# Folded sums of eight rows kept to the end of a mixture-of-experts layer, and the strips of two weight transfers asked for separately

## The chip, the cores and the metric

The kernel runs on one core of one Trainium2 chip. The metric is the device time of one execution, in microseconds (us). All inputs, weights and outputs are float32.

## What is computed

One layer of a decoder for 256 prompt rows and 8 sample rows (264 in all), each of 1024 columns. Its first part (a short convolution and retention) takes the first 166 us and is not touched, apart from a table of constants. The rest is this, with 32 experts of which each row uses 4:

```python
logits = x @ w_router + b_router
gates = softmax(top_4(logits))
h = xb @ w_up[e] + b_up[e]                         # w_up[e] is 1024 x 2048, 8 MB
act = min(h_glu, 7) * sigmoid(1.702 * h_glu) * (clip(h_lin, -7, 7) + 1)
y_rows = act @ w_down[e] + b_down[e]               # w_down[e] is 1024 x 1024, 4 MB
h = h + sum over k of gates[k] * y[k]
y_out = h * rsqrt(mean(h * h) + 1e-6) * norm_final
```

The kernel also returns the states of the first part.

## The kernel before

**The stream of weights.** Each expert has four chunks of `w_up` ("u", 2 MB each) and two of `w_down` ("d", 2 MB each): 192 chunks (`LAST`) in the order u of expert n, then d of expert n - 1. They go through a ring of ten slots of 2 MB (`ring_all`, chunk s in slot s % 10). SyncE (SP) issues all these transfers, each as soon as TensorE (PE) has used what stood in the slot (`mm_done`), so that some 30 us of work always stands in the DMA queue. From expert 8 to the start of expert 28 two neighbouring chunks are one transfer of 4 MB (`pairs`, L569; 128 rows of 32 KB). Before and after these come single chunks (L582), then halves (L540), and the last expert's `w_down` comes in four parts of 1 MB (L575, rows of pieces of 2 KB). A transfer counts as landed when its semaphore has all 16 increments, from all DMA engines that carry it.

**An expert's work on PE.** `ups(n)` multiplies 64 gathered rows with `w_up[n]` in eight steps j (L1035). Between the steps stand the gathering for the next expert (L1009, L1017, L1027) and, after three of them, `combine(n - 2, c)`: it multiplies the gates, spread over the rows, with the expert's 64 results (`y_rows`) for rows 0 to 127 (c = 0), 128 to 255 (c = 1) and the 8 sample rows (c = 2). VectorE (DVE) adds what it gives to `h_tok` (L1887). `downs(n - 1)` follows (L1054).

**The eight sample rows.** For experts 0 to 25 (`FOLD` = 26) combine has a folded form for c = 2: the 1024 columns of the eight rows lie as 4 groups of 32 partitions by 2 x 128 columns, eight matmuls of 128 columns give them (L1095), and DVE adds them to a tile `sums` (L1884). At expert 26 eight matmuls with the identity bring `sums` back into plain rows (L1107), and from then on combine uses the plain form for c = 2, two matmuls of 512 columns on 8 rows (L1102). The biases' term `gates @ b_down` is added at experts 20 to 22 (`bias(c)`, L1140), for c = 2 in the plain form too.

**The end.** `downs_last` handles the last expert's `w_down` in two halves of columns, p = 0 and p = 1 (L1114, eight steps j each). combine(30, c) stands between the steps of p = 0; `combine_last(0, c)` (L1129) stands after steps 1 and 4 of p = 1 for c = 0 and 1, and after the last step for c = 2, followed by `combine_last(1, c)` for c = 0, 1, 2. DVE adds each (`add_last`, L1954). ScalarE (ACT) squares each half row (L1470), GpSimd (POOL) multiplies the left halves with `norm_final` (L652, once `g_fin` is loaded, L584) and takes the roots of the mean squares (`last_root`, L656, L658: first for c = 0, then for c = 1 and 2 together, once all three are squared). ACT scales the left halves (L1533), DVE the right ones (L1997), and SP stores three blocks (L596, L599).

Of the kernel before, what the change touches and what calls it, by code (L numbers as in the profile page):

```python
# [13 lines left out]
P = 128  # L14
# [33 lines left out]
PAIRED = (8, 28)  # L48
LAST = E * CPR
TOK = [(0, 128), (128, 128), (256, NS)]  # L50
# [7 lines left out]
def hybrid_layer(nc, x_prompt, x_sample, state_conv, state_ret, norm_mix, w_in, conv_w, ret_norm, w_out,  # L58
# [17 lines left out]
    with ExitStack() as top:  # L76
# [76 lines left out]

        pairs = [s for s in range(place["u", PAIRED[0], 0], place["u", PAIRED[1], 0], 2) if s % RING < RING - 1]
        signal, seen = [], [0] * RING
        for s in range(LAST):
            if s - 1 in pairs:
                signal.append(signal[s - 1])
                continue
            seen[s % RING] += 1  # L160
            signal.append((s % RING, 16 * seen[s % RING]))

        with ExitStack() as ph:
# [183 lines left out]
            gt = lay(6304, T)[P - E:P]  # L347
            g_fin = lay(5280, D)
# [6 lines left out]
            weighted = [h_rows[:, 0:512], h_rows[:, 512:1024], xg[0:NS, :]]  # L355
# [3 lines left out]
            early_in = sem("early_in")  # L359
# [29 lines left out]
            last_in = [sem(f"last_in{p}") for p in range(2)]  # L389
            fin_part = sem("fin_part")  # L390
            fin_eps = sem("fin_eps")
            weighed_again = sem("weighed_again")
            fin_redone = sem("fin_redone")
# [42 lines left out]
            FOLD = 26  # L436

            def ring(s):
                r = s % RING
                return ring_a[:, r, :] if r < FIRST else ring_b[:, r - FIRST, :]  # L440

# [9 lines left out]
            def half_signal(s):  # L451
                return s % RING, 16 * sum(h % RING == s % RING for h in halved if h <= s)

# [25 lines left out]
            def _(sp):  # L479
# [17 lines left out]
                for j in range(2, 2 * len(ORDER) + 4):  # L497
# [12 lines left out]
                    if j >= 3:  # L510
# [5 lines left out]
                        if j % 2 and k == STASHED:  # L516
                            sp.dma_start(ring_a[:, k, 0:2 * FF], chunk_src(stream[k])[:, 0:2 * FF]).then_inc(landed[k], 16)
                            sp.dma_start(ring_a[:, k, 2 * FF:4 * FF],
                                         chunk_src(stream[k + RING])[:, 2 * FF:4 * FF]).then_inc(early_in, 16)
# [34 lines left out]
                for s in range(RING, LAST):  # L554
# [23 lines left out]
                    if s in halved:  # L578
# [19 lines left out]
                sp.wait_ge(fin_rows, 3)  # L598
                sp.dma_start(y_sample.rearrange("b s d -> (b s) d"), h_tok[0:NS, 2, :]).then_inc(stored, 16)  # L599
                sp.wait_ge(stored, 48)  # L600
# [3 lines left out]
            def _(pool):  # L604
# [43 lines left out]
                pool.wait_ge(late_in, 32)  # L648
                for c in range(CT):
                    pool.wait_ge(comb_added, CT * (E - 1) + c + 1)  # L650
                    n = TOK[c][1]
                    pool.tensor_tensor(weighted[c], h_tok[0:n, c, 0:512], g_fin[0:n, 0:512],  # L652
                                       ALU.mult).then_inc(fin_weighted, 1)
                def last_root(c0, c1, i):
                    pool.wait_ge(fin_ssq, c1)
                    pool.tensor_tensor(st[:, 6 + c0:6 + c1], st[:, c0:c1], st[:, 3 + c0:3 + c1], ALU.add).then_inc(fin_chain, 1)  # L656
                    pool.wait_ge(fin_chain, i + 1)
                    pool.tensor_tensor(st[:, 6 + c0:6 + c1], st[:, 6 + c0:6 + c1],  # L658
                                       minus_half[:].broadcast_to([P, c1 - c0]), ALU.pow).then_inc(fin_scale, 1)

                pool.wait_ge(fin_eps, 1)
                last_root(0, 1, 0)
                last_root(1, CT, 1)

            @block.tensor
            def _(pe):
# [398 lines left out]
                def combine(n, c):  # L1065
# [19 lines left out]
                    else:  # L1085
                        pe.wait_ge(comb_added, CT + CT * n + c)
                        if c == 0:
# [3 lines left out]
                    if c == 2 and isinstance(n, int) and n < FOLD:  # L1091
                        for g in range(4):
                            for half in range(2):
                                at = slice(half * CAP, (half + 1) * CAP)
                                mm = pe.matmul(bank[32 * g:32 * g + 32, C + half, 0:P], spread[at, n % 2, t0:t0 + 32],  # L1095
# [971 lines left out]
```

## Time and profile before

| | |
|---|---|
| median of three runs | 1082.04 us (1081.49 to 1084.55) |
| the profiled execution, its own time | 1081.66 us |
| its span, first to last instruction | 1079.8 us |
| TensorE busy | 1065.2 us, 99% of the span |
| VectorE, ScalarE, GpSimd busy | 361.4, 152.8, 11.9 us |
| granted TensorE clock, mean of the span | 0.998 of full |
| weights and the rest moved by DMA | 431.47 MB, mean 400 GB/s |

The profiled execution's time is 1.86 us above its span, which is what lies around the instructions, and 0.38 us under the median of the three runs. A busy share of 99% doesn't tell that PE sets the time: its weights come at the pace of the DMA engines, and the stretches in which one or the other is ahead have to be read apart.

### The profile page before, as it was taken

Reading aid. Unit: us, or ns where it says so; the run is one execution under the profiler, and the core shown is the slowest. Engines: PE = TensorE matmul, PEld = TensorE weight load, DVE = VectorE, ACT = ScalarE, POOL = GpSimd, SP = SyncE. Lnnn points to the kernel's source line nnn. Section 1 sums busy time; section 2 is a strip of 40 time slices with the busy share of each in tenths; the row PEclk is TensorE's granted clock in tenths of the full one; section 3 lists DMA queues with packets and bytes.
Section 4 is the critical chain, followed back from the end, with each engine's and each line's share of the span. In section 5 each row is a group of like instructions: output and inputs, shape, how many; then the busy total and the mean of one; then the engine's idle time right before and its main releaser. Section 6 shows DMA issues by size and latency. Waiting matters only on the chain.

```text
span 1079.8 us, 13215 instructions
## 1 busy us (share of the span) xinstructions
PE 1065.2 (99%) x5687; PEld 445.8 (41%) x5688; DVE 361.4 (33%) x572; ACT 152.8 (14%) x302; POOL 11.9 (1%) x28
## 2 busy tenths in 40 slices
PE   9999999999999999999999999999999999999997
PEld 7888664333333333333333333333333333333332
DVE  3376534233322233332222233323232232232234
ACT  2121144111111101111111110011111101101113
POOL 1000010000000000000000000000000000000002
PEclk9999999999999999999999999999999999999999
DMA  8875969999999999999999999999999999999995
GB/s 291 305 276 199 402 214 390 419 425 426 427 429 433 431 430 429 433 427 434 429 429 429 434 431 430 429 429 432 433 432 427 432 430 433 423 427 428 424 413 188
DMA packets 45515, 431.47 MB, mean 400 GB/s; under 512 B 4968, under 2 KB 20364, under 8 KB 25872
## 3 DMA queue, kind: packets, MB, share of 16 engines
q1 hardware_dynamic: 44848, 430.41, 95.3%
q8 instruction: 46, 0.75, 0.3%
q10 hardware_dynamic: 608, 0.20, 0.1%
q14 instruction: 13, 0.11, 0.0%
HBM read 427.00 MB, written 3.48 MB: 399 GB/s over the span
## 4 chain that ended last, share of the span: by engine, by line
PE 87%; DMA 11%; issue 0%; ACT 0%; DVE 0%; POOLq 0%; DVEq 0%; ACTq 0%; POOL 0%
PE bank L1035 39%; PE bank L1054 16%; DMA ring_all<-in_w_up 10%; PE bank L716 9%; PE bank L1102 6%; PE bank L1009 4%; PE bank L1046 2%; PE bank L826 2%; PE bank L1017 2%; PE bank L1027 1%; PE bank L1095 1%; PE bank L669 1%; PE bank L1114 1%; DMA ring_all<-in_w_in 1%; PE bank L834 1%; PE bank L1140 1%
## 5 line engine op out<-in xcount | busy, mean ns | idle before, releaser
L1035 PE MATMUL bank<-ring_all,work 128*64 128x512 f32 x2040 | 482.9, 600 | 4.9 <-DMA ring_all<-in_w_up 4.9
L1035 PEld LDWEIGHTS bank<-ring_all,work 128*64 128x64 f32 x2040 | 133.9, 136 | 253.4 <-issue 243.9
L1054 PE MATMUL bank<-ring_all,work 128*64 128x512 f32 x992 | 225.3, 596 | 0.0
L1887 DVE TENSOR_TENSOR h_tok<-h_tok,bank 128x1024 f32<-128x1024 f32 (+1 forms) x67 | 81.7, 1220 | 234.2 <-PE bank L1102 228.3
L1054 PEld LDWEIGHTS bank<-ring_all,work 128*64 128x64 f32 x992 | 68.4, 137 | 128.1 <-issue 128.0
L716 PE MATMUL bank<-work,ring_all 128*128 128x264 f32 x384 | 87.1, 387 | 0.5 <-DMA ring_all<-in_w_in 0.5
L716 PEld LDWEIGHTS bank<-work,ring_all 128*128 128x128 f32 x384 | 72.3, 190 | 13.1 <-DMA ring_all<-in_w_in 1.1
L1857 DVE TENSOR_TENSOR work<-bank,bias_up 128x1024 f32<-128x1024 f32 x32 | 39.2, 1224 | 113.9 <-PE bank L1046 113.9
L1102 PE MATMUL bank<-work 64*128 64x512 f32 (+1 forms) x268 | 75.1, 637 | 0.0
L1874 DVE TENSOR_TENSOR work<-work 128x512 f32<-128x512 f32 x32 | 22.2, 692 | 106.5 <-ACT work L1453 106.4
L1437 ACT ACTIVATE work<-bank 128x264 f32<-128x264 f32 x32 | 12.5, 391 | 313.1 <-PE bank L1027 313.1
L1445 ACT ACTIVATE shared<-bank 128x512 f32<-128x512 f32 x64 | 34.7, 595 | 118.4 <-PE bank L1035 118.4
L1459 ACT ACTIVATE work<-bank 128x512 f32<-128x512 f32 x31 | 18.5, 597 | 218.3 <-PE bank L1054 218.3
L1009 PE MATMUL bank<-x_tok,pick_b 128*64 128x512 bf16 x372 | 45.6, 379 | 0.0
L1884 DVE TENSOR_TENSOR work<-work,bank 128x256 f32<-128x256 f32 x26 | 11.0, 421 | 90.4 <-PE bank L1095 90.4
L1102 PEld LDWEIGHTS bank<-work 64*128 64x128 f32 (+1 forms) x268 | 19.2, 177 | 53.1 <-issue 51.5
L1846 DVE TENSOR_TENSOR work<-bank,vec 128x512 f32<-128x512 f32 x31 | 21.4, 692 | 58.2 <-PE bank L1017 43.3
L1046 PEld LDWEIGHTS bank<-ident,shared 128*128 128x128 f32 x256 | 27.4, 141 | 25.9 <-ACT shared L1445 23.5
L1431 ACT ACTIVATE work<-bank 128x512 f32<-128x512 f32 x31 | 18.5, 597 | 125.4 <-PE bank L1009 125.4
L1009 PEld LDWEIGHTS bank<-x_tok,pick_b 128*64 128x64 bf16 x372 | 22.7, 110 | 29.8 <-issue 18.2
L1046 PE MATMUL bank<-ident,shared 128*128 128x128 f32 x256 | 35.0, 280 | 0.0
L1017 PEld LDWEIGHTS bank<-ident,work 128*128 128x128 f32 x124 | 17.4, 210 | 25.2 <-issue 25.2
(238 smaller groups left out, 550.6 us busy)
## 6 DMA issues: line engine op xcount, KB each, us to landing
ring_all<-in_w_up SPq DMA_DIRECT2D x40, 4096.0 KB, 33.5
ring_all<-in_w_down SPq DMA_DIRECT2D x20, 4096.0 KB, 34.5
ring_all<-in_w_up SPq DMA_DIRECT2D x33, 2048.0 KB, 15.2
ring_all<-in_w_down SPq DMA_DIRECT2D x15, 2048.0 KB, 18.4
ring_all<-in_w_up SPq DMA_DIRECT2D x29, 1024.0 KB, 10.4
ring_all<-in_w_down SPq DMA_DIRECT2D x18, 1024.0 KB, 11.9
ring_all<-in_w_in SPq DMA_DIRECT2D x13, 1024.0 KB, 5.0
ring_all<-in_w_out SPq DMA_DIRECT2D x4, 1024.0 KB, 11.6
```

The source lines that it names most:

```text
L716: mm = pe.matmul(bank[:, i % 4, 0:T], w_ring[:, slot, k, m % 2 * P:(m % 2 + 1) * P], xnt[:, k, :] if j else x_raw[:, k, :], start=(k == 0) ...
L826: mm = pe.matmul(bank[:, 2 * c + n, :], mix_in[:, k, c * P:(c + 1) * P], wo_slot[i][:, a, :], start=(late == 0 and a == 0), stop=(late == ...
L1009: mm = pe.matmul(bank[half * CAP:(half + 1) * CAP, X, :], marks, rows[:, half * 512:(half + 1) * 512], start=(i == 0), stop=(i == len(part ...
L1017: mm = pe.transpose(bank[:, X, j * P:(j + 1) * P], xg[:, j:j + 4 * P - 3:4], ident[:])
L1035: mm = pe.matmul(bank[half * CAP:(half + 1) * CAP, up_bank(n) + b, :].rearrange("q (k p) -> q p k", k=KT), x, src[half][:, b * 512:(b + 1) ...
L1046: mm = pe.transpose(bank[:, HT + j // 4, j % 4 * P:(j % 4 + 1) * P], h_rows[:, j * P:(j + 1) * P], ident[:])
L1054: mm = pe.matmul(bank[half * CAP:(half + 1) * CAP, Y, :], av[:, 2 * i + k, :], src[:, k * D + half * 512:k * D + (half + 1) * 512], start= ...
L1102: mm = pe.matmul(bank[0:m, at_bank + half, :], spread[at, n % 2 if isinstance(n, int) else 0, t0:t0 + m], y_rows[at, :], start=True, stop= ...
L1445: nc.scalar.activation(h_rows.rearrange("p (k b q) -> p b k q", k=KT, b=2)[:, b], bank[:, up_bank(n) + b, :].rearrange("p (k q) -> p k q", ...
L1857: tt(hb[:].rearrange("p h j s -> p j h s"), bank[:, HT:HT + 2, :].rearrange("p a (j h s) -> p (a j) h s", h=2, s=CAP), bias_up[:, e, :, :] ...
L1874: tt(out[:], sig[:], hb[:, 1], ALU.mult).then_inc(act_ready, 1)
L1887: tt(rows, rows, bank[0:m, b:b + 2, :], ALU.add).then_inc(comb_added, 1)
```

## The change

Four things change.

1. The eight sample rows stay folded for all experts. At expert 0 eight matmuls with the identity put the rows' own values into the folded sums; `bias(2)`, the last two experts and the overflow rounds use the folded form; the eight matmuls of expert 26 (L1107) are gone. The sum of squares over the four groups of partitions is taken by two matmuls of one column with a constant 128 x 128 matrix (`same_row`), at the very end of PE's program (`join_rows`).
2. At the end the order is (0,0), (0,1), (0,2), (1,2), (1,0), (1,1) for (p, c), and the first three stand after steps 1, 3 and 5 of p = 1. The prompt rows' two stores come as before; the sample rows are stored folded by four transfers of 8 rows x 2 x 128, two on SP and two on ACT. POOL no longer weighs the sample rows; DVE scales them in one instruction of 128 x 256.
3. `g_fin`, a folded copy of `norm_final` (four transfers of 8 rows) and `same_row` are loaded into the ring slot of chunk 186, after PE has used it, in place of `g_fin` alone in `work`.
4. Two transfers of 4 MB, those of steps 4 to 7 of experts 16 and 25, leave out the last 768 and 512 columns (3 and 2 KB of each row). These strips are asked for by three more transfers each, of 69, 57 and 2 rows.

```diff
+UNEVEN = {(16, 2): 768, (25, 2): 512}
+FEW_ENGINES = (slice(0, 69), slice(69, 126), slice(126, 128))
+LATE = LAST - 6
...
-            seen[s % RING] += 1
+            seen[s % RING] += 1 + (len(FEW_ENGINES) if s in uneven else 0)
...
-                        sp.dma_start(ring_all[:, s % RING:s % RING + 2, :].rearrange("p a n -> p (a n)"),
-                                     pair_src(stream[s])).then_inc(landed[s % RING], 16)
+                        pair = ring_all[:, s % RING:s % RING + 2, :].rearrange("p a n -> p (a n)")
+                        cut = 8 * FF - uneven.get(s, 0)
+                        sp.dma_start(pair[:, 0:cut], pair_src(stream[s])[:, 0:cut]).then_inc(landed[s % RING], 16)
+                        if s in uneven:
+                            for few in FEW_ENGINES:
+                                sp.dma_start(pair[few, cut:], pair_src(stream[s])[few, cut:]).then_inc(landed[s % RING], 16)
...
-                sp.wait_ge(comb_psum, CT * (FOLD + 1))
+                sp.wait_ge(mm_done, LATE + 1)
+                sp.dma_start(same_row, c_square[:, 8, :]).then_inc(late_in, 16)
                 sp.dma_start(g_fin[:], norm_final.rearrange("(a d) -> a d", a=1)
                              .partition_broadcast(P)[:, 0, :]).then_inc(late_in, 16)
+                for g in range(4):
+                    sp.dma_start(g_fold[32 * g:32 * g + NS], norm_final.rearrange("(a n g t) -> g a n t", a=1, n=2, g=4)[g]
+                                 .partition_broadcast(NS)[:, 0]).then_inc(late_in, 16)
...
-                pool.wait_ge(late_in, 32)
-                for c in range(CT):
+                pool.wait_ge(late_in, 112)
+                for c in range(2):
...
-                    if c == 2 and isinstance(n, int) and n < FOLD:
+                    if c == 2:
...
-                            if p == 1 and j in (1, 4):
-                                combine_last(0, j // 4)
-                    combine_last(0, 2)
-                    for c in range(CT):
-                        combine_last(1, c)
+                            if p == 1 and j in (1, 3, 5):
+                                combine_last(j // 2)
+                    for i in range(CT, 2 * CT):
+                        combine_last(i)
...
+                pe.wait_ge(late_in, 112)
+                pe.wait_ge(fin_part, CT)
+                pe.wait_ge(fin_sel, 1)
+                join_rows()
```

On SP, in the middle of the stream, each expert had three transfers of 4 MB before (`ring_all` is the ring, 128x8192 a pair of chunks, line 569): two of `w_up`, one of `w_down`. This stands for expert 16 with the change (line 584 is what line 569 was, line 587 is new):

```order
L584 DMA ring_all<-in_w_up 128x8192
L584 DMA ring_all<-in_w_up 128x7424
L587 DMA ring_all<-in_w_up 69x768
L587 DMA ring_all<-in_w_up 57x768
L587 DMA ring_all<-in_w_up 2x768
L584 DMA ring_all<-in_w_down 128x8192
```

Expert 16's second pair has lost 768 columns, and three transfers behind it bring them; all four count on the pair's semaphore.

On PE, the second half of the last expert (L1114 is `down_last`, L1129 `combine_last`), before:

```order
L1129 MATMUL bank<-work 128x256 [waits comb_added]
L1129 MATMUL bank<-work 128x256
L1114 MATMUL bank<-ring_all,work 64x256 x6
L1129 MATMUL bank<-work 8x256 [waits comb_added]
L1129 MATMUL bank<-work 8x256
L1129 MATMUL bank<-work 128x256 [waits spread_copied,y_copied,comb_added]
L1129 MATMUL bank<-work 128x256
L1129 MATMUL bank<-work 128x256 [waits comb_added]
L1129 MATMUL bank<-work 128x256
L1129 MATMUL bank<-work 8x256 [waits comb_added]
L1129 MATMUL bank<-work 8x256
```

and with the change (L1137 is `down_last`, L1154 and L1159 `combine_last` for the sample and the prompt rows, L1311 the join):

```order
L1154 MATMUL bank<-work 32x128 [waits comb_added]
L1154 MATMUL bank<-work 32x128 x3
L1137 MATMUL bank<-ring_all,work 64x256 x4
L1154 MATMUL bank<-work 32x128 [waits spread_copied,y_copied,comb_added]
L1154 MATMUL bank<-work 32x128 x3
L1159 MATMUL bank<-work 128x256 [waits comb_added]
L1159 MATMUL bank<-work 128x256
L1159 MATMUL bank<-work 128x256 [waits comb_added]
L1159 MATMUL bank<-work 128x256
L1311 MATMUL bank<-work,ring_all 128x1 [waits fin_sel,fin_part,late_in]
L1312 MATMUL bank<-work,ring_all 128x1
```

The sample rows' first combine has moved ahead of the last two steps, their second to the front of the last three, and the join stands behind all.

On SP, the end of the program before (the last weights, `norm_final`, the load of the greatest count, and the stores behind the branches of the overflow rounds):

```order
L575 DMA ring_all<-in_w_down 128x4x512 x4
L584 DMA work<-in_norm_final 128x1024
L459 TENSOR_LOAD most
...
L596 DMA out<-h_tok 128x1024 x2
L599 DMA out<-h_tok 8x1024
```

and with the change:

```order
L592 DMA ring_all<-in_w_down 128x4x512 x4
L601 DMA ring_all<-in_c_square 128x128
L602 DMA ring_all<-in_norm_final 128x1024
L605 DMA ring_all<-in_norm_final 8x2x128 x4
...
L617 DMA out<-h_tok 128x1024 x2
L620 DMA out<-work 16x1x128 x2
```

Five loads have come behind the last weights on this queue, and two short stores stand where one was; ACT has two more like them at its end.

## Rows read from the trace of the kernel before

**Rows 1.** The page: the span, the engines' busy time.

```profile
span 1079.8 us, 13215 instructions
PE 1065.2 (99%) x5687; PEld 445.8 (41%) x5688; DVE 361.4 (33%) x572; ACT 152.8 (14%) x302; POOL 11.9 (1%) x28
```

**Rows 2.** Sums by stretch: bounds, length, busy time by engine, clock, DMA share, GB/s.

```profile
650.00:850.00 200.00, 198.60 (x1045) 69.67 (x1041) 59.59 (x87) 22.33 (x42) 0.00 (x0) 1.00 1.00 431
```

**Rows 3.** The waits of PE: line, releaser, total us, times, longest.

```profile
PE bank L1035 <- DMA ring_all<-in_w_up: 4.9, 5, 1.2
```

**Rows 4.** PE in order of time, experts' first steps: start, length, what, idle.

```profile
857.82 3.65 PE L1035 MATMUL bank<-ring_all,work 128*64 128x512 f32 x16 [1.18 <-DMA ring_all<-in_w_up]
...
916.10 3.65 PE L1035 MATMUL bank<-ring_all,work 128*64 128x512 f32 x16 [1.18 <-DMA ring_all<-in_w_up]
```

**Rows 5.** The chain that ended last, one piece: start, length, what.

```profile
877.79 38.17 DMA ring_all<-in_w_up
```

**Rows 6.** Line 575 in 1030 to 1032 us: the transfer, and its time to landing.

```profile
L575 SPq DMA_DIRECT2D ring_all<-in_w_down x1: 3189/3189/3189, 1030.5 to 1030.5; - x1
DMA to landing us min/median/max: 27.0/27.0/27.0
```

**Rows 7.** Sums by stretch at the end of the stream, columns as in rows 2.

```profile
1059.00:1060.00 1.00, 1.00 (x8) 0.30 (x6) 0.26 (x1) 0.00 (x0) 0.00 (x0) 1.00 1.03 395
1060.00:1061.00 1.00, 1.00 (x10) 0.48 (x8) 0.96 (x1) 0.00 (x0) 0.00 (x0) 1.00 0.78 301
...
1062.00:1063.00 1.00, 1.00 (x10) 0.36 (x8) 1.00 (x1) 0.00 (x0) 0.00 (x0) 1.00 0.59 219
...
1065.00:1066.00 1.00, 1.00 (x10) 0.45 (x6) 0.00 (x0) 0.19 (x1) 0.00 (x0) 1.00 0.29 115
1066.00:1067.00 1.00, 1.00 (x12) 0.60 (x10) 0.69 (x1) 0.00 (x0) 0.00 (x0) 1.00 0.00 0
```

**Rows 8.** PE in order of time: the forms of combine and bias.

```profile
616.45 0.45 PE L1095 MATMUL bank<-work 64*32 64x128 f32 x16
616.83 1.94 PE L1035 MATMUL bank<-ring_all,work 128*64 128x512 f32 x8
...
791.90 1.88 PE L1140 MATMUL bank<-h_tok,work 32*8 32x512 f32 x4
793.71 1.09 PE L1046 MATMUL bank<-ident,shared 128*128 128x128 f32 x8
...
961.45 1.03 PE L1102 MATMUL bank<-work 64*8 64x512 f32 x4
962.41 1.91 PE L1107 MATMUL bank<-work,ident 128*8 128x128 f32 x16
964.26 1.94 PE L1035 MATMUL bank<-ring_all,work 128*64 128x512 f32 x8
```

**Rows 9.** All engines in order of time, the end: start, length, what, idle.

```profile
1057.55 1.08 PE L1114 MATMUL bank<-ring_all,work 128*64 128x256 f32 x8
...
1067.13 1.29 POOL L652 TENSOR_TENSOR shared<-h_tok,work 128x512 f32<-128x512 f32 x1 [905.17 <-DVE h_tok L1954]
...
1069.71 2.69 PE L1129 MATMUL bank<-work 64*8 64x256 f32 x16
...
1070.36 2.17 DVE L1954 TENSOR_TENSOR h_tok<-h_tok,bank 8x512 f32<-8x512 f32 x3 [1.29 <-PE bank L1129]
...
1073.53 0.63 ACT L1470 ACTIVATE work<-h_tok 8x512 f32<-8x512 f32 x1
...
1074.60 0.70 POOL L658 TENSOR_TENSOR work<-work,minus_half 128x2 f32<-128x2 f32 x1
...
1075.33 1.40 DVE L1997 SCALAR_TENSOR_TENSOR h_tok<-h_tok,work 128x512 f32<-128x512 f32 x2 [0.96 <-POOL work L658]
...
1076.76 0.35 SPq L599 DMA_DIRECT2D out<-h_tok  x1
```

More of the change, by code:

```diff
@@ L154, in hybrid_layer @@
         pairs = [s for s in range(place["u", PAIRED[0], 0], place["u", PAIRED[1], 0], 2) if s % RING < RING - 1]
+        uneven = {place["u", e, j]: cols for (e, j), cols in UNEVEN.items()}
         signal, seen = [], [0] * RING
@@ L597, in _ @@
                 sp.wait_ge(fin_ready, 3)
-                sp.wait_ge(fin_rows, 3)
-                sp.dma_start(y_sample.rearrange("b s d -> (b s) d"), h_tok[0:NS, 2, :]).then_inc(stored, 16)
-                sp.wait_ge(stored, 48)
+                for g in range(2):
+                    sp.dma_start(y_folded(g), sums[32 * g:32 * g + NS]).then_inc(stored, 16)
+                sp.wait_ge(stored, 96)
                 sp.wait_ge(out_done, 16 * 3)
@@ L1090, in combine @@
                         pe.sem_inc(pe_passed, 1)
-                    if c == 2 and isinstance(n, int) and n < FOLD:
+                    slot = n % 2 if isinstance(n, int) else 0
+                    if c == 2:
+                        if isinstance(n, int) and n == 0:
+                            for g in range(4):
+                                for half in range(2):
+                                    pe.matmul(bank[32 * g:32 * g + 32, C + half, 0:P], ident[0:NS, 0:32],
+                                              h_tok[0:NS, 2, half * 512 + g * P:half * 512 + (g + 1) * P], start=True, stop=False)
                         for g in range(4):
@@ L1139, in bias @@
                     for half in range(2):
-                        mm = pe.matmul(bank[0:m, C + half, :], gt[:, t0:t0 + m], b_down_sb[:, half * 512:(half + 1) * 512],
-                                       start=True, stop=True)
+                        if c == 2:
+                            for g in range(4):
+                                mm = pe.matmul(bank[32 * g:32 * g + 32, C + half, 0:P], gt[:, t0:t0 + 32],
+                                               b_down_sb[:, half * 512 + g * P:half * 512 + (g + 1) * P], start=True, stop=True)
+                        else:
+                            mm = pe.matmul(bank[:, C + half, :], gt[:, t0:t0 + m], b_down_sb[:, half * 512:(half + 1) * 512],
+                                           start=True, stop=True)
                     mm.then_inc(bias_psum, 1)
@@ L1468, in square_part @@
                 def square_part(p, c, done):
[L1469 to L1470 removed]
+                    rows = sums[:, p, :] if c == 2 else h_tok[:, c, p * 512:(p + 1) * 512]
+                    nc.scalar.activation(sig[:].rearrange("p j s -> p (j s)")[:, 0:P if c == 2 else 512], rows,
                                          ACT.Square, scale=D ** -0.5,
[L1472 removed]
+                                         accum_out=st[:, 3 * p + c:3 * p + c + 1]).then_inc(done, 1)
                 for n in range(E):
@@ L1892, in add_bias @@
                     dve.wait_ge(comb_added, CT * (BIAS + c - 2) + c + 1)
-                    rows = h_tok[0:m, c, :].rearrange("p (a b) -> p a b", a=2)
-                    tt(rows, rows, bank[0:m, C:C + 2, :], ALU.add).then_inc(bias_added, 1)
+                    if c == 2:
+                        tt(sums, sums, bank[:, C:C + 2, 0:P], ALU.add).then_inc(bias_added, 1)
+                        return
+                    rows = h_tok[:, c, :].rearrange("p (a b) -> p a b", a=2)
+                    tt(rows, rows, bank[:, C:C + 2, :], ALU.add).then_inc(bias_added, 1)
                 nc.vector.memset(st[:], 0.0)
@@ L1980, in overflow @@
                     activate(n, None)
-                    for c in range(CT):
-                        add(CT + CT * n + c, c)
+                    for i, c in enumerate(LASTS):
+                        add(CT + CT * n + i, c)
                 def weigh_again(k):
                     dve.wait_ge(comb_added, k * CT + SUMS)
-                    dve.wait_ge(fin_weighted, CT)
-                    for c in range(CT):
+                    dve.wait_ge(fin_weighted, 2)
+                    for c in range(2):
                         ins = weigh(c)
```

194 lines of the change are left out of this document (109 added, 85 removed).

## The prediction

> **What bounds the kernel now.** The page comes first: PE is busy 99% of the span [rows 1]. That looks like a kernel bound by PE. The sums by stretch say something else as well: the DMA engines' share is 1.00 and they move 431 GB/s [rows 2], so PE and DMA are both full. Which is ahead decides what a saving is worth, so I read the waits of PE: five waits for `w_up`, 4.9 us in all, 1.2 at most [rows 3]. In order of time, experts 25 and 27 start 58.28 us apart, at 857.82 and 916.10, each just after such a wait [rows 4]: 29.14 us for an expert's 12 MB (12.58e6 bytes) is 432 GB/s, the DMA's own rate. So in this stretch the stream sets the pace, and PE catches up with it each time; the chain that ended last goes through such a transfer, 38.17 us long and asked for at 877.79 [rows 5]. After 916 no wait is shown. But the first part of the last `w_down`, asked for at 1030.5, takes 27.0 us to land, that is until 1057.5 [rows 6], and PE begins its step at 1057.55 [rows 9]. So there, 22 us before the end, the stream is still level with PE. A saving on PE ahead of 1057.5 is given back by a wait for weights, unless the stream gets earlier too. What comes behind 1057.55 is a tail of small work, one engine handing over to the next, and there each saving counts.
>
> The stream's end shows how the 16 engines stand. Their share is full until 1060, 0.78 in the next us, 0.59 from 1062 to 1063, 0.29 from 1065 to 1066, and nothing after 1066 [rows 7]. 0.59 of 16 is nine engines: some seven are done between 1060 and 1062, nine between 1064 and 1066.5. Each transfer is cut evenly among them, yet it counts as landed only with the last one. So seven engines lead by 4 to 6 us, and the lag of the rest is lost time for PE.
>
> **The change part by part.** The sum is made against the profiled execution, 1081.66 us, which is 0.38 under the median.
>
> The folded form costs 616.83 - 616.45 = 0.38 us on PE, the plain one 962.41 - 961.45 = 0.96 [rows 8]: 0.58 less for each of experts 26 to 30, 2.9 in all. The unfolding of expert 26 took 964.26 - 962.41 = 1.85, `bias(2)` 793.71 - 791.90 = 1.81 against some 0.4 now. Expert 0 gets eight short matmuls more, about as many columns as a folded combine, so 0.4 at most. Sum 2.9 + 1.9 + 1.4 - 0.4 = 5.8 us of PE, all but the 0.58 of expert 30 ahead of 1057.55. What hides them is the stream: if it didn't get earlier they would turn into waits, and I count them as nothing. Without that cover they would be worth 5.2 us.
>
> The strips. Per engine the rate is 431 / 16 = 26.9 GB/s. 3 KB of 128 rows are 393 KB, 24.6 KB or 0.91 us for each of 16 engines; 2 KB are 0.61 us. If the strips go to engines that lead, the others land everything behind the second strip 1.52 us earlier. The leaders pay. 128 rows go to 16 engines as eight each; if an equal share of rows is what makes the split, 69 and 57 rows can only go to three engines (23 and 19 each) and 2 rows to two. The pieces are small: with pieces of 2 KB the stream runs at 395 GB/s [rows 7], 24.7 per engine. So (393 + 262) / 3 / 24.7 = 8.8 us, less the 1.5 that they are spared, is 7.3 us more on each of three engines. Their lead is 4 to 6 us as rows 7 show it, and more in truth, since the last transfers were let into the queue late (the issue of the first of them took 3.2 us [rows 6], against 0.35 of line 599 [rows 9]) and the leaders ran dry. So after both strips the three are about the last ones: with a lead of 8 the stream's end comes 0.7 earlier, with 6 it comes 1.3 later. The bounds for this term are -1.5 (all the lead is there) and +1.3. I take -0.5, a lead just under 8, between the two, since the dry queue cuts off what rows 7 can show of it.
>
> The Trainium skill, "DMA: Bandwidth & Descriptors", section "Why a DMA increments its semaphore by 16 and not by 1", states that the number of engines is the largest one up to 16 that divides the slowest dimension on both sides, and that SP's transfers use the lowest-numbered ones. By that 69 and 57 rows go to three engines and 2 rows to two, always the same ones, which would make the sum above; by its "Rules for kernel authors", parts of a transfer that each spray over all 16 gain nothing, which would make it zero. No row here shows which engines lead.
>
> Issuing six more transfers takes SP time that nobody waits for; some 30 us of work stand in the queue.
>
> The tail, from the last step of PE on. Before: PE's last four combines start at 1069.71 and end at 1072.40, DVE's three first adds run 1070.36 to 1072.53 and the fourth follows, ACT's last square starts at 1073.53, POOL's last root runs 1074.60 to 1075.30, DVE scales 1075.33 to 1076.73, SP's last store is issued at 1076.76 and the span ends 3.0 later [rows 1, 9]. Now the first sample combine lies between two steps (+0.2 on PE, four matmuls in place of eight) and no longer behind them, and expert 30's is 0.58 shorter: the last step ends 0.4 earlier. Behind it come a short combine (0.2), a short add (under 0.4, 128 x 128) and then the two prompt blocks. DVE has three adds in place of four, the one on the chain short: the last add that POOL's second root needs ends 2.4 us after the last step in place of 3.5. ACT's square of the sample rows, 0.63 and 0.2 for the sum before, no longer stands behind the other two. So the second root ends 1.1 us earlier relative to the step. Behind it DVE has 0.7 for block 1 as before, and 0.4 in place of 0.65 for the samples. Then two stores of the samples on SP one after the other, and two on ACT beside them: this costs one issue more, 0.35 to 0.8 us (line 599 took 0.35). Net behind the last step: 0.3 to 1.1 earlier, I take 0.9. With the 0.4 the tail gives -1.3.
>
> Price of the new waits: the join on PE waits for `late_in`, with nothing behind it but the branch; its two matmuls of one column and the add on DVE end before ACT's second square does. POOL's first weighing (1.29 us a block, started at 1067.13 before, when DVE's first sum was there [rows 9]) waits for five more loads, which land behind the last weights, about 1067; its two blocks are done before 1070, and the root behind them is not due before 1071, so there's 1 us of slack.
>
> Sum: 0 - 0.5 - 1.3 = -1.8, so 1079.9 for the profiled time, 1080.2 for the median.
>
> **The rivals.**
> 1. The strips fall on engines that lag. Nothing in the rows excludes it: nine of sixteen lag. Then the last engine's stream ends up to 7.3 us later, and PE first waits for it at expert 26, behind the second strip. Less the tail's 1.3, and up to 2 us where a strip's engine isn't quite the last one, it's 4 to 6 us slower: 1084.4 to 1086.5, say 1086. It decides once one of the strips' engines leads by less than 3.5 us. Chance 0.17.
> 2. The strips change nothing, since they are shared out over all engines or the lead is just eaten up: only the tail remains, 1080.7; where the leaders end 1.3 later, 1082.0. Chance 0.25.
> 3. The full lead is there: stream -1.5, tail -1.3 to -1.6, so 1078.6 to 1079.2. The folded sums then also show, since PE needs them to keep up. Chance 0.15.
> 4. The tail gets worse: late loads or four short stores whose landings queue up, +1 to 1.5 in place of -0.9. Near 1082. Chance 0.05.
>
> **How the numbers follow.** The forecast (gain of 1 to 2.5 us) has 0.38. A change of under 0.3%, 3.2 us, can't be told from none by measuring this kernel. Within it lie the forecast, rivals 2 and 4 and most of rival 3; faster needs rival 3 in full and some of the runs' own spread (0.13); slower is rival 1 and a little of 2 (0.19). The range leaves out half of rival 3's lower part and the slower part of rival 1: 1078.4 to 1085.6.
>
> **What would show it.** Sums by stretch behind 1060: a share that stays near 1 longer and falls within 2 us, the end at 1065 to 1066, would show that the strips went to leaders. PE's waits for `w_up` at experts 20 to 25 shorter or no longer between waits (starts at 857 in place of 857.82), and possibly one longer at expert 26 or 27. No line for the unfolding; all c = 2 combines of 0.38. Waits of PE for weights also behind 1000, where none are now: the 5.8 us given back. From the first step of the last `w_down` to the end 21.0 us in place of 22.3. The prediction is wrong if that step starts later than 1058.5 (rival 1), or if the tail isn't shorter.

## The result

The changed kernel takes 1089.97 us (median of 6 runs, 1089.01 to 1091.4) beside 1081.51 us for the kernel before (6 runs, 1080.96 to 1084.55): ratio 1.0071, 95% interval 1.0057 to 1.0084. It is slower by 8.5 us. The forecast was 1080.2, a gain, with a range of 1078.4 to 1085.6; the measured time lies above the range, and "slower" had been given a chance of 0.19.

The page of the changed kernel: the span, the engines' busy time, and the traffic in 40 equal slices of 27.2 us:

```profile
span 1088.9 us, 13396 instructions
PE 1064.6 (98%) x5771; PEld 448.2 (41%) x5772; DVE 356.1 (33%) x574; ACT 151.4 (14%) x301; POOL 11.0 (1%) x27
GB/s 284 307 276 208 407 214 364 422 425 427 427 429 432 431 429 432 430 433 429 431 432 428 378 432 432 428 432 429 434 431 428 424 405 426 427 427 428 423 402 174
```

The span is 9.1 us longer than in [rows 1]. PE isn't busier (1064.6 beside 1065.2), its idle time grew from 14.6 to 24.3 us. Two slices drop out of a level of about 430 GB/s, the 23rd (378, from 599 us) and the 33rd (405, from 871 us): the places of the two strips. Next the waits of PE, then two pieces of PE in order of time (start, length, what, idle before), then four sums by stretch (columns as in [rows 2]), all of the changed kernel:

```profile
PE bank L1058 <- DMA ring_all<-in_w_up: 12.3, 9, 4.8
PE bank L1137 <- DMA ring_all<-in_w_down: 0.8, 1, 0.8
```

```profile
877.26 3.42 PE L1058 MATMUL bank<-ring_all,work 128*64 128x512 f32 x8 [4.77 <-DMA ring_all<-in_w_up]
...
1066.24 1.08 PE L1137 MATMUL bank<-ring_all,work 128*64 128x256 f32 x8 [0.78 <-DMA ring_all<-in_w_down]
```

```profile
596.00:612.00 16.00, 16.00 (x82) 5.68 (x80) 6.22 (x10) 1.71 (x3) 0.00 (x0) 1.00 1.00 337
...
874.00:876.00 2.00, 0.00 (x0) 0.00 (x0) 0.00 (x0) 0.00 (x0) 0.00 (x0) 1.00 1.03 330
876.00:878.00 2.00, 0.74 (x4) 0.29 (x6) 0.00 (x0) 0.00 (x0) 0.00 (x0) 0.89 0.83 347
878.00:880.00 2.00, 2.00 (x8) 0.38 (x4) 0.00 (x0) 0.00 (x0) 0.00 (x0) 0.50 1.18 508
```

For comparison, the first stretch in the kernel before:

```profile
596.00:612.00 16.00, 16.00 (x82) 5.42 (x78) 4.32 (x7) 1.71 (x3) 0.00 (x0) 1.00 1.00 429
```

The waits for `w_up` went from 4.9 us [rows 3] to 12.3, and one alone, at expert 25's strip, is 4.77. During the 16 us around the first strip the DMA share stays at 1.00 but the traffic is 337 GB/s; in the same stretch of the kernel before it is 429. The engines have work all the time and each piece takes longer: (429 - 337) x 16 / 431 = 3.4 us of the stream are lost.

At the second strip, from 868 to 884 us, the traffic is 367 in place of 431. The trace's records of single pieces show that the others are slowed too, and all of them: from 600 to 604 us each piece of 32 KB took 1.89 to 2.09 us, where it took 1.22 before the strip. The pair's semaphore got 24 increments in the trace, 16 for the large transfer and eight for the strip, as three, three and two engines would give.

Behind the wait of 4.77 us the granted clock is 0.50 of full, the lower of the two levels, and the next eight matmuls take 3.42 us, where the same step takes 1.94 in [rows 8]. The first step of the last `w_down` starts at 1066.24 in place of 1057.55 [rows 9]: 8.7 of the 9.1 us are there, ahead of the tail. The remaining 0.4 is the tail, 22.66 from that step to the end in place of 22.25.

### The profile page after: what moved, and what is told of

It reads as the page before. It is cut to its first block, busy times and chain, and to the rows that moved or that the text cites. A ratio compares the mean times of both kernels' runs of the same rounds, so it can differ in the third digit from the quotient of the medians.

```text
span 1088.9 us, 13396 instructions
## 1 busy us (share of the span) xinstructions
PE 1064.6 (98%) x5771; PEld 448.2 (41%) x5772; DVE 356.1 (33%) x574; ACT 151.4 (14%) x301; POOL 11.0 (1%) x27
## 4 chain that ended last, share of the span: by engine, by line
PE 81%; DMA 17%; SPq 0%; issue 0%; DVE 0%; POOLq 0%; ACT 0%; POOL 0%; DVEq 0%; ACTq 0%
PE bank L1058 35%; PE bank L1077 15%; DMA ring_all<-in_w_up 14%; PE bank L739 9%; PE bank L1130 5%; PE bank L1032 4%; DMA ring_all<-in_w_down 3%; PE bank L1069 2%; PE bank L849 2%; PE bank L1040 2%; PE bank L1050 1%; PE bank L1124 1%; PE bank L692 1%; PE bank L1137 1%; PE bank L857 1%; SPq L553 0%
## 5 line engine op out<-in xcount | busy, mean ns | idle before, releaser
L1058 PE MATMUL bank<-ring_all,work 128*64 128x512 f32 x2040 | 485.0, 602 | 12.4 <-DMA ring_all<-in_w_up 12.3
L1937 DVE TENSOR_TENSOR h_tok<-h_tok,bank 128x1024 f32<-128x1024 f32 x62 | 75.7, 1221 | 227.1 <-PE bank L1130 227.1
L1130 PE MATMUL bank<-work 64*128 64x512 f32 x248 | 70.2, 643 | 0.0
L1130 PEld LDWEIGHTS bank<-work 64*128 64x128 f32 x248 | 18.9, 186 | 50.2 <-issue 48.6
```

Source lines behind the costliest of these rows:

```text
L1058: mm = pe.matmul(bank[half * CAP:(half + 1) * CAP, up_bank(n) + b, :].rearrange("q (k p) -> q p k", k=KT), x, src[half][:, b * 512:(b + 1) ...
L1130: mm = pe.matmul(bank[:, at_bank + half, :], spread[at, slot, t0:t0 + m], y_rows[at, :], start=True, stop=True)
L1937: tt(rows, rows, bank[:, b:b + 2, :], ALU.add).then_inc(comb_added, 1)
```

## The experiments

Sixteen kernels were run. They are told by what they separate. The numbers in parentheses are a ratio to the kernel before and its 95% interval. The kernel before was timed again beside each group of them, with medians of 1082.58 to 1083.42, so the ratios compare better than the times do.

### Folding without strips, and strips without folding

```diff
-UNEVEN = {(16, 2): 768, (25, 2): 512}
+UNEVEN = {}
```

> The change without its strips (all 4 MB transfers whole). Theory A: the strips carry the whole loss and the folded sums change nothing but the tail, which the changed kernel shows 0.4 us longer (22.66 against 22.25 us from the first step of the last w_down): the stream sets that step's start as before, so +0.4 us, 1081.9, within 0.3%. Theory B (my prediction's sum): the tail is 1.3 us shorter, 1080.2. Rival C: the folded sums themselves cost the stream time (four small loads of 8 rows, a table of constants): over 1085.

Measured 1082.29 (1.000, 0.999 to 1.0011). Two lines of its page and its waits of PE:

```profile
PE 1060.5 (98%) x5771; PEld 446.6 (41%) x5772; DVE 356.0 (33%) x574; ACT 151.4 (14%) x301; POOL 11.0 (1%) x27
...
PE bank L1058 <- DMA ring_all<-in_w_up: 8.0, 9, 1.2
PE bank L1137 <- DMA ring_all<-in_w_down: 0.8, 1, 0.8
PE bank L1077 <- DMA ring_all<-in_w_down: 0.6, 1, 0.6
```

PE is busy 4.7 us less than in [rows 1], and waits 9.4 us for weights in place of 4.9: the saving is there and is given back, but for 0.2 us. The strips alone, put into the kernel before (the same `UNEVEN`, `FEW_ENGINES` and three transfers):

> The kernel before with the strips alone. Theory A: both strips slow the whole stream, 3.5 and 2.3 us on the mean of the engines as the changed kernel shows, and the three engines that take them end later than the last did: the last w_down's first step starts near 1066.2, 8 to 9 us later than before, 1090. Rival: the strips only shift load between engines, 1081.5 to 1083. Beside each strip the traffic should fall to 140 to 310 GB/s for some 8 us.

Measured 1090.23 (1.0066, 1.0042 to 1.0091), traffic of 324 GB/s from 596 to 612 us, and

```profile
PE bank L1042 <- DMA ring_all<-in_w_up: 11.4, 7, 4.8
```

So the strips are the whole loss. One strip only, in the changed kernel:

```diff
-UNEVEN = {(16, 2): 768, (25, 2): 512}
+UNEVEN = {(16, 2): 768}
```

> The kernel after with the strip of (25, 2) left away: (25, 2) is one whole transfer again, (16, 2) keeps its 3 KB strip by 69, 57 and 2 rows. If the two strips cost by their own delays alone (3.5 and 2.3 us of mean landing time of the 16 engines), 1085.5 to 1087.5. If what costs is mainly that a second loss meets a stream without a lead (the wait of 4.77 us at expert 25, then a clock of 0.57), 1083 to 1085.

Measured 1085.3 (1.0031, 1.0018 to 1.0045). The first strip costs 3.4 us by its ratio, as much as the stream lost in those 16 us; the second, though smaller, the other 4.3. That lies between the two expectations: most of the loss adds up, and the second strip costs some 2 us more than the 2.3 by which it delays the mean landing. The slow matmuls behind the long wait (1.5 us more than usual in the row above) may be a part of that. This was not separated further.

### What it is in the strips

The first experiments varied how the strip is cut up. All of these are the kernel before with strips of 3 and 2 KB at the same two pairs: by one transfer of all 128 rows (all16), by two of rows 0 to 63 and 64 to 127 (halves), by two of 119 and 9 rows (seven), and by the three of 69, 57 and 2 rows, but read from one contiguous stretch (contig):

```diff
 three kernels, with FEW_ENGINES in place of the slices of 69, 57 and 2 rows:
+FEW_ENGINES = (slice(0, 128),)                   # all16
+FEW_ENGINES = (slice(0, 64), slice(64, 128))     # halves
+FEW_ENGINES = (slice(0, 119), slice(119, 128))   # seven
 and with 69, 57 and 2 rows, read from one contiguous stretch of w_up (contig):
+source = w_up[0, stream[s][1], 0:width // 2, :].rearrange("r n -> (r n)").rearrange("(p w) -> p w", w=width)
```

> The same strips (the last 3 and 2 KB of each row), asked for by one transfer of 128 rows each, so that they are cut over all engines, eight rows each. Theory R (reading): pieces that lie 32 KB apart in memory are what slows everybody, whoever asks: traffic falls beside the strips as in the changed kernel, and the loss is some 3 to 6 us. Theory W (few engines): it is that three engines carry 43 small pieces each: then nothing is lost here but the price of small pieces, under 0.3 us, and the time is that of before, 1081.5.

> The strips by 69, 57 and 2 rows into the same places, but read from one contiguous stretch of the same expert's w_up (so these columns hold other weights; nothing else is changed). Theory R: with the pieces side by side in memory the traffic doesn't fall, and what stays is the overload of three engines: 1082 to 1084. Theory W: the same loss as with the strips where they belong, 1089 to 1090.

> [...] Theory P (place): it is writing outside the own eight rows that slows all: traffic falls beside the strips, for about 1 us a strip since the pieces are few, and pieces take 0.2 us in place of 0.12. Theory F (few): it is that the small pieces fall on few engines; then nothing changes against the transfer of 128 rows: pieces of 0.12 us, the time of before, 1082.

> The strips by transfers of 119 and 9 rows. If the equal split of rows holds, seven engines take 17 rows each and nine take one row: some 27 KB (1.0 us) and 18 KB (0.7 us) more for each of the seven leaders, which lead by more than 2 us. Without contention the other nine land 1.4 us earlier and the time falls by 1 to 1.5 us, 1081. With contention as in the strips of three engines (pieces of 0.2 us, all others slowed): each piece falls on 7 engines at once, the stretch is 17 pieces long (3.5 us) and the stream loses 1 to 3 us a strip: 1083 to 1087.

Sums by stretch from 596 to 612 us, in the order all16, contig, halves, seven:

```profile
596.00:612.00 16.00, 16.00 (x82) 5.46 (x80) 4.02 (x6) 1.71 (x3) 0.00 (x0) 1.00 1.02 435
...
596.00:612.00 16.00, 16.00 (x84) 5.52 (x78) 5.52 (x10) 1.71 (x3) 0.00 (x0) 1.00 1.01 345
...
596.00:612.00 16.00, 16.00 (x82) 5.56 (x80) 5.00 (x9) 1.71 (x3) 0.00 (x0) 1.00 1.01 349
...
596.00:612.00 16.00, 16.00 (x84) 5.42 (x80) 5.16 (x9) 1.71 (x3) 0.00 (x0) 1.00 1.00 343
```

The times were 1082.34 (1.0, 0.9987 to 1.0013), 1090.9 (1.0076, 1.005 to 1.0101), 1087.36 (1.0045, 1.0028 to 1.0061) and 1089.86 (1.0071, 1.0052 to 1.0089). A strip asked for by one transfer of 128 rows costs nothing, so small pieces as such are harmless. Reading from a contiguous stretch changes nothing. And halves cost too, though all 16 engines carry each of them (48 increments in the trace for the pair and the two halves of its strip): fewness of engines can't be all of it. The strips by 119 and 9 rows cost more than was expected of them, 1089.86 beside 1083 to 1087.

Then whole rows of 32 KB, to take the small pieces out altogether: 112 rows by the main transfer, 9 and 7 by two more.

```diff
+UNEVEN = {(16, 2): 112, (25, 2): 112}
+FEW_ENGINES = (slice(112, 121), slice(121, 128))
...
+first = uneven.get(s, P)
+sp.dma_start(pair[0:first], pair_src(stream[s])[0:first]).then_inc(landed[s % RING], 16)
```

> No strips of columns: the same two pairs are asked for as 112 rows (seven for each of 16 engines) and then 9 and 7 whole rows of 32 KB, so seven engines carry one row more than the even share and seven one row less, in pieces of 32 KB. Theory S (small pieces do the harm): traffic stays at 431 GB/s and the laggards land 2.4 us earlier after both; the time falls by up to 2 us if the leaders take the rows, 1080. Theory P or F: traffic falls beside the 16 rows as it does beside the strips, packets of 32 KB take over 1.5 us in place of 1.22, and the time is 1082 to 1086.

Measured 1122.16 (1.0365, 1.0347 to 1.0383): five times the loss of the strips, with big pieces only, where 1086 had been the most expected. The traffic there is half of what it was:

```profile
590.00:610.00 20.00, 20.00 (x104) 7.37 (x102) 6.22 (x10) 2.80 (x5) 0.00 (x0) 1.00 1.02 211
```

What all costly kernels share, and the harmless one doesn't, is that a transfer covers only a part of the 128 rows of the ring, and so cuts them in another place. That gave theory P: it matters to which rows (partitions) an engine writes. Suppose that rows are dealt out in order, in equal shares; no view shows which engine writes which rows, so this is an assumption. Then a transfer of 128 rows gives engine k rows 8k to 8k + 7 each time. Two transfers of even and odd rows leave every engine in its eight. Two halves don't (engine k gets rows 4k to 4k + 3, then 64 + 4k to 64 + 4k + 3), at the same count of transfers, bytes and pieces. Both were tried on the strips, and on the two whole pairs of 4 MB, (16, 2) and (25, 2), with no strips and all pieces of 32 KB:

```diff
 the strips:
-FEW_ENGINES = (slice(0, 64), slice(64, 128))
+FEW_ENGINES = (slice(0, 128, 2), slice(1, 128, 2))
 whole pairs of 32 KB rows, halves, then even/odd:
+PARTS = (slice(0, 64), slice(64, 128))
+PARTS = (slice(0, 128, 2), slice(1, 128, 2))
...
+for half in PARTS if s in uneven else (slice(0, P),):
+    sp.dma_start(pair[half], pair_src(stream[s])[half]).then_inc(landed[s % RING], 16)
```

> The kernel before with both strips asked for by two transfers of 64 rows, the even rows and the odd rows, instead of rows 0 to 63 and 64 to 127. [...] Theory P (it costs when an engine writes rows that are another engine's in the whole transfers): 1081.5 to 1083, within 0.1% of the kernel before, and 3 KB packets of about 121 ns with traffic near 431 GB/s. Rival N (two transfers more, or packets of 4 rows for each engine, cost by their number): as the halves, 1087 to 1088.

> [...] Theory P: those 4 MB move at about half the rate, as in the kernel with 112 + 9 + 7 rows (205 to 221 GB/s), some 9 to 10 us lost at each pair, 1095 to 1120. Rival U (it was the unequal count of rows per engine, 9 beside 7, and the few engines of the small transfers): none of that is left here, 1081.5 to 1084.

> [...] Theory P: within 0.15% of the kernel before, traffic stays near 431 GB/s through both pairs. Rival N (the number of transfers or their rows per engine costs): as the whole halves.

Strips by even and odd rows: 1082.11 (0.9994, 0.9981 to 1.0007). Whole pairs by halves: 1114.87 (1.0294, 1.0267 to 1.0321), by even and odd rows 1082.76 (0.9994, 0.9978 to 1.001). Sums by stretch: 596 to 612 us of the strips by even and odd rows, then 590 to 610 of the whole halves, then of the whole even and odd rows:

```profile
596.00:612.00 16.00, 16.00 (x81) 5.44 (x78) 4.42 (x6) 1.71 (x3) 0.00 (x0) 1.00 1.02 434
```

```profile
590.00:610.00 20.00, 18.74 (x96) 6.84 (x92) 6.48 (x10) 2.80 (x5) 0.00 (x0) 1.00 1.01 215
```

```profile
590.00:610.00 20.00, 20.00 (x116) 7.05 (x114) 6.22 (x10) 2.80 (x5) 0.00 (x0) 1.00 1.01 433
```

Same bytes, same number of transfers and pieces, 215 against 433 GB/s.

### Writing or reading, and which rows

The halves also differ from the even and odd rows in where in DRAM each transfer reads. So writing and reading were crossed (in `PARTS` the rows written stand first, the rows read second):

```diff
 to_halves:
+PARTS = ((slice(0, 64), slice(0, 128, 2)), (slice(64, 128), slice(1, 128, 2)))
 to_even_odd:
+PARTS = ((slice(0, 128, 2), slice(0, 64)), (slice(1, 128, 2), slice(64, 128)))
...
+sp.dma_start(pair[half], pair_src(stream[s])[rows_in_w]).then_inc(landed[s % RING], 16)
```

> The kernel before with two pairs asked for by two transfers of 64 rows, written to rows 0 to 63 and 64 to 127, but read from the even and the odd rows of the weights (the weights of two experts' steps so stand in other rows, and the output for them is another one). If what costs is where the rows are written: as the whole halves, 1110 to 1117, 590 to 610 us at about 215 GB/s. If it is how DRAM is read: as the kernel before, 1081 to 1084, 431 GB/s.

> The other way round: written to the even and the odd rows, read from rows 0 to 63 and 64 to 127 (here too the weights of two experts' steps stand in other rows). Writing decides: 1081 to 1084, 431 GB/s. Reading decides: 1110 to 1117, 215 GB/s.

Written to halves 1114.48 (1.0293, 1.0254 to 1.0332), written to even and odd rows 1082.64 (0.9995, 0.9984 to 1.0006). From 590 to 610 us, in this order:

```profile
590.00:610.00 20.00, 20.00 (x116) 7.08 (x114) 6.22 (x10) 2.80 (x5) 0.00 (x0) 1.00 1.00 215
```

```profile
590.00:610.00 20.00, 20.00 (x104) 7.41 (x102) 6.45 (x10) 2.80 (x5) 0.00 (x0) 1.00 1.01 432
```

Where the rows are written decides, where they are read makes no difference (half rows against even and odd ones). Why it does has two forms left: an engine leaves its own eight rows, or one transfer reaches only some of the places through which rows are written. The Trainium skill has the second form: "SBUF — State Buffer", section "Door 1: The DMA port swizzle", gives the 128 partitions to 16 ports in groups of four rows, with row p and row p + 32 on the same one and row p + 64 on another. By it rows 0 to 63 reach eight ports and even rows all sixteen, which would halve the rate in the one and leave it in the other; the 215 and 433 GB/s measured here agree. Rows 32 to 95 also reach all sixteen, but by the assumption above they lie as far from each engine's eight as a half does:

```diff
+PARTS = (slice(32, 96), slice(0, 32), slice(96, 128))
```

> The kernel before with two pairs asked for whole by transfers of rows 32 to 95, then 0 to 31, then 96 to 127. The Trainium skill, 'SBUF - State Buffer', section 'Door 1: The DMA port swizzle', lays partitions on 16 ports of which rows 0 to 63 reach eight and rows 32 to 95 all sixteen. Theory of ports: the first 2 MB of a pair move at about 431, the other 2 MB at about 215 GB/s; half of what the whole halves lost, so 1094 to 1101. Theory of an engine's own eight rows (rows 8k to 8k+7): in rows 32 to 95 the engines are as far from their own rows as in the halves, so all 4 MB go at 215 and it comes to 1110 to 1117.

Measured 1102.13 (1.0183, 1.0159 to 1.0207): 1.1 us above the interval of the ports (1094 to 1101), 8 under that of an engine's own eight (1110 to 1117). Sums by stretch of this kernel, then of the whole halves:

```profile
589.00:592.00 3.00, 3.00 (x18) 1.01 (x16) 0.42 (x1) 1.06 (x2) 0.00 (x0) 1.00 1.04 448
...
613.00:616.00 3.00, 2.59 (x6) 0.77 (x8) 0.00 (x0) 0.00 (x0) 0.00 (x0) 0.57 1.04 448
```

```profile
589.00:592.00 3.00, 3.00 (x16) 0.83 (x12) 0.08 (x1) 1.08 (x2) 0.00 (x0) 1.00 1.03 229
...
613.00:616.00 3.00, 0.00 (x0) 0.00 (x0) 0.00 (x0) 0.00 (x0) 0.00 (x0) 0.50 0.87 218
```

The halves are slow from about 588 until 616 us, 28 us for 4.2 MB that would need 19.5 us at half rate; the middle version only from 592 until 612. The semaphores' increments say the same engine by engine. The seven engines that lead took 9.8 us for their share of the first 2 MB as rows 0 to 63 (first increments at 588.5 and 598.3 us), but 4.9 us as rows 32 to 95 (588.6 and 593.5), which is the full rate.

Why the slow stretch is longer than the pair is read from the same increments: in the halves' kernel the first engine enters the pair at 588.5 us and the last one leaves it at 617.3, since up to 9 us lie between the first and the last engine's end of one transfer. While one engine is still in the pair, the pieces of all the others, who are already in the next whole transfer, are slow as well. For the same reason, it seems, the middle rows got less than their full gain: the nine engines behind needed some 7 us for them, while the leading ones were already in rows 0 to 31.
Last, the strips by three engines as in the change, but with rows spread over nearly the whole tile:

```diff
-FEW_ENGINES = (slice(0, 69), slice(69, 126), slice(126, 128))
+FEW_ENGINES = (slice(0, 114, 2), slice(1, 114, 2), slice(114, 128))
```

> The kernel before with the two strips asked for by 57 even rows of 0 to 112, 57 odd rows of 1 to 113 and rows 114 to 127: the first two go to three engines (19 rows each) as the 69 and 57 rows did, but each is spread over nearly all rows. Theory of writing place alone: within 0.2% of the kernel before, 596 to 612 us above 410 GB/s. If three engines alone cost: as the strips of 69, 57 and 2 rows, 1088 to 1091, 324 to 345 GB/s in that stretch. In between if both do.

Measured 1086.42 (1.0046, 1.0031 to 1.0061), 354 GB/s from 596 to 612 us beside 337 of the changed kernel. It fits neither theory, it lies between: some two thirds of the loss (0.46 of 0.66 to 0.71%) stay when the rows are spread. The ports alone don't explain this, nor the strips of the change: by the map three engines write through three ports at a time at most, yet from 600 to 604 us each 32 KB piece of the other transfers took 1.70 to 1.85 us here and 1.89 to 2.09 us in the changed kernel, 1.22 otherwise. So it is shown that strips cut this way slow the whole stream; by which path three engines slow all the others stays open.

### The tail

In the changed kernel the second sample combine, moved between two steps, no longer stands behind the last step. PE in order of time at that place, with ACT's copy that it waits for:

```profile
1077.31 1.08 PE L1137 MATMUL bank<-ring_all,work 128*64 128x256 f32 x8
...
1078.44 0.38 ACT L1509 ACTIVATE work<-bank 128x256 f32<-128x256 f32 x1 [0.94 <-PE bank L1137]
...
1078.92 0.42 PE L1154 MATMUL bank<-work 64*32 64x128 f32 x8 [0.53 <-issue]
```

PE's first combine behind the steps needs `y`, which ACT copies after the last step; in the kernel before, combine (0, 2) lay over this copy, now PE idles 0.53 us. So that combine was put back behind the last step, in the kernel without strips:

```diff
-if p == 1 and j in (1, 3, 5):
-    combine_last(j // 2)
+if p == 1 and j in (1, 4):
+    combine_last(j // 4)
...
-for i in range(CT, 2 * CT):
+for i in range(CT - 1, 2 * CT):
```

> The change without strips, with the third combine of p = 0 put back behind the last step of p = 1 (and the two others after steps 1 and 4, as before). Theory: in the changed kernel PE stands 0.5 us behind the last step since the next combine waits for ACT's copy of y, and the third combine, which used to fill this gap, costs 0.6 us between the steps. Put back, the tail from the first step of the last w_down is 0.5 us shorter than without strips (22.7): 22.1 to 22.2. Rival: the stores behind it set the end, nothing changes. The times alone can't tell: 1081.5 to 1082.5.

Measured 1082.03 (0.9995, 0.9985 to 1.0005). In its profile the first step of the last `w_down` begins at 1061.14 and the span ends at 1083.3: 22.16 in place of 22.66, as expected. Against the kernel before (22.25) this is next to nothing: the second root ends 0.7 us earlier after that step, and the stores take it back. The end of the changed kernel, all engines in order of time:

```profile
1081.88 0.55 POOL L678 TENSOR_TENSOR work<-work,minus_half 128x1 f32<-128x1 f32 x1
...
1082.69 1.08 POOL L678 TENSOR_TENSOR work<-work,minus_half 128x2 f32<-128x2 f32 x1
1083.28 1.68 SPq L617 DMA_DIRECT2D out<-h_tok  x2
...
1083.81 0.75 DVE L2053 SCALAR_TENSOR_TENSOR h_tok<-h_tok,work,ring_all 128x512 f32<-128x512 f32 x1 [0.59 <-POOL work L678]
1084.48 0.48 DVE L2060 SCALAR_TENSOR_TENSOR work<-work,ring_all 128x256 f32<-128x256 f32 x1
1084.99 2.36 ACTq L1584 DMA_DIRECT2D out<-work  x2
1085.00 1.52 SPq L620 DMA_DIRECT2D out<-work  x2
```

## Why the prediction was wrong

**Stream and PE are level until 1057.5, and a saving on PE is given back.** Right. 4.7 us less of PE work, 4.5 us more of waits, time unchanged (1.000).

**The size of the saving, 5.8 us.** It was 4.7 by the busy time; the term was worth nothing either way.

**The strips, -0.5 with bounds -1.5 and +1.3.** This is the step that failed: "(393 + 262) / 3 / 24.7 = 8.8 us, less the 1.5 that they are spared, is 7.3 us more on each of three engines", and above all what stood unsaid beside it, that the other thirteen go on at 26.9 GB/s each and "land everything behind the second strip 1.52 us earlier". The total traffic was taken as fixed, only shared out otherwise. The runs show that it isn't fixed: 337 GB/s in place of 429 for 16 us at the first strip, 367 in place of 431 at the second, and the pieces of the other engines slow with those of the three. The split itself was guessed right (24 increments). Which rows a transfer covers decides whether this happens: the same strips by one transfer of 128 rows or by even and odd rows cost nothing, by halves 0.45%. For the strips of the change that is a part of the cause at most, since two thirds of the loss stayed with the rows spread. The price of a piece, 24.7 GB/s per engine, came from transfers of 128 rows, and so was no bound for transfers of 69 and 57. The loss was 7 to 8 us, outside the bounds of -1.5 and +1.3.

**Rival 1 (the strips' engines lag), 1084.4 to 1086.5.** The times don't follow from its own words: 4 to 6 us above 1082.0 are 1086.0 to 1088.0, so the range's upper end, 1085.6, left out all of this rival and not only its slower part. It is the nearest in sign and size, not in cause. It has one or a few engines late at the end; the trace shows all of them slowed at both strips, and a halved rate also where all 16 had equal work (whole halves). The sign by which it was to be told, a first step later than 1058.5, came true for another reason.

**The rule weighed in the prediction.** By the Trainium skill, "DMA: Bandwidth & Descriptors", section "Rules for kernel authors", splitting a tile in two partition halves isn't worth it, since both spray over the same 16 engines. I read this as "costs nothing". Here it costs 4.9 us by the strips' halves (0.45%) and 31.8 us by the whole halves of two pairs (2.94%); where a page and a measurement differ, the measurement decides. With even and odd rows, which also split the tile in two, it costs nothing.

**The tail, -1.3.** Wrong by 1.7: +0.4. Three terms. "The last step ends 0.4 earlier": it ended 12.15 us after the first one of the last `w_down` in place of 12.22, and PE then idled 0.53 us for ACT's copy, which combine (0, 2) had covered; I costed the move without asking what that combine hid. "The second root ends 1.1 us earlier relative to the step": it ended 0.2 earlier (17.53 after the first step of the last `w_down`, 17.75 before [rows 9]), for that wait and because the root took 1.08 us in place of 0.70, beside a DVE scaling that starts 0.23 us before it (whether the scaling is the reason was not tested). "One issue more, 0.35 to 0.8 us": the two issues on each engine took 1.52 on SP and 2.36 on ACT, so the last one ends 2.4 us after DVE's last work, where line 599 took 0.35 in all. The late loads and the join cost nothing, as said.

## What to carry to other kernels

Where a bulk load in a full stream must be cut, cut it along the columns with all 128 rows, or by even and odd rows, both of which measured as nothing here; transfers of contiguous halves ran at half the rate, and a few engines with a strip of their own slowed all the others. A profile shows this kind of loss as a DMA share of 1.00 with fewer GB/s, so read both columns: a busy share isn't bandwidth. Before moving work out from between two dependent steps, ask what it covers there.

## What the runs showed of the hardware

- Two transfers of 64 contiguous rows move 4 MB at 215 GB/s, the even and the odd rows at 433; the place of writing makes this difference, not that of reading (215 and 432 with the two crossed).
- The disturbance reaches past the transfer: with the whole halves the rate stays down for 28 us in place of 19.5, for as long as one of the engines, 9 us apart, is in the pair.
- A strip of 3 KB pieces that only three engines carry slows the pieces of all the others: 32 KB took 1.89 to 2.09 us in place of 1.22.
- Transfers of 69, 57 and 2 rows gave eight increments of the semaphore, as three, three and two engines would; those of 119 and 9 rows gave sixteen.
- The kernel with 112 + 9 + 7 rows also fell to 211 GB/s, and that from the start of the transfer of 112 rows. By the map of the Trainium skill ("SBUF — State Buffer", "Door 1: The DMA port swizzle") 112 rows reach all sixteen ports, the last four of the odd ones with half their rows. That map alone would leave most of the rate; why it was halved stays open, and so does what share of the three engines' loss is their fewness (354 GB/s with rows spread, 337 without).
- After PE had idled 4.77 us the granted clock stood at the lower level (0.50) from 878 to 880 us, and one step took 3.42 us in place of 1.94.
- A root of two columns on POOL took 1.08 us beside a DVE operation of 128 x 512 and 0.70 without one [rows 9]; that the one comes of the other is not shown.
